# Gathering the last two chunks of four output tiles into one unit in two mixers, a gate's sigmoid from exponential and logarithm, and a bank claimed later

## The chip, the cores and the metric

The kernel runs on one core of one Trainium2 chip. The metric is the device time of one execution in microseconds; the runs of the kernel before lie at 2596.78, 2597.88 and 2606.25, with a median of 2597.88. Five engines work side by side and are tied by semaphores: TensorE (PE; its weight loads are shown as PEld), VectorE (DVE), ScalarE (ACT), GpSimd (POOL) and SyncE (SP), which issues transfers.

## The reference

Two blocks run one after the other on 512 tokens of width 1024, in float32. The first has two layers; the change touches only it.

```python
for layer in range(DEPTH):                       # DEPTH = 2
    h = modulate(rms_norm(x, mix_norm[layer]), sh1, sc1)
    y = ab_mixer(...) if layer % 2 == 0 else cd_mixer(...)
    x = x + g1 * y
    h = modulate(rms_norm(x, ffn_norm[layer]), sh2, sc2)
    x = x + g2 * swiglu(h, ffn_w1[layer], ffn_w2[layer])
# ab_mixer: four gated-linear-attention heads, four sparse attention heads
o_gla = rms_norm(o_gla, out_norm) * silu(gr)     # gr: 4 tiles of [128, 512]
return concat([o_gla, o_dsa]) @ w_out            # [512, 1024] @ [1024, 1024]
# cd_mixer: four pooled groups, four stick-breaking attention heads
return concat([o_pool, o_sb]) @ w_out            # the same shape
```

## The kernel before, in words

**Weights.** All large weights come as one stream of units. A unit is 128 x 1024 floats (512 KB); for the output product of a mixer it holds one output tile's eight chunks of 128 x 128, one per 128 channels of the input. SP loads units in order into a ring of four slots (L1254), each after the slot's last product has raised its `emptied` semaphore. POOL splits a unit into an upper half (L1828) and a lower half (L1831). TensorE then makes each chunk as three products of 128 x 512 (`products`, L384 to L386): upper by high, upper by low, lower by high. Only after the lower half may it begin the unit.

**The output product of a mixer** (`first_mix_out`, `second_mix_out`) has eight output tiles in two passes of four, one PSUM bank for each tile of a pass. In the first pass TensorE goes over the four tiles with their first chunks while the last attention heads are still being computed; these heads are the last chunks. So all four slots of the ring are held until the last chunk of the first pass, and the first unit of the second pass is loaded and split after that. In the first mixer the chunks go in the order `MIX_ORDER = (4, 5, 0, 1, 6, 2, 3, 7)`, five of them early (`MIX_EARLY`), the other three at the end. In the second, four chunks are early, then chunks 4 and 5, then 6, then 7.

**The heads.** Steps are numbered h, two to each weight tile: `late_part(h)` (first mixer) and `sb_part(h)` (second) put attention work between the halves of a tile's products. In the first mixer, step 24 to 27 lie between the early chunks of the output product. ACT takes the gate tiles `gr` from PSUM with a Copy, and after steps 20 and 24 makes Silu of two of them each; Silu needs another table than Exp and Ln, so a table load stands before and after (`gate_silu`, `tables`). `SB_AT` and `SB_OUT_AT` say at which steps the scores and outputs of the four stick-breaking heads stand.

**Behind the product.** DVE adds each output tile to the residual (L1939), ACT squares and scales it, DVE splits it again (L1900, L1901): one chain of eight tiles. TensorE needs all eight squares in `square_sum` (L414, L416), after half of the first FFN tile. The first FFN pass has four tiles; then a loop makes the rest (`ffn`). Before this loop, in layer 0, TensorE claims bank 7 for the sums of `late_sum`. DVE frees that bank with `bias_sum` of the second pair of tiles (L1973).

## Time and profile before

| | us |
|---|---|
| median of 3 runs | 2597.88 |
| profiled execution | 2600.07 |
| its span | 2598.3 |
| TensorE busy in it | 2516.0 (97%) |
| POOL busy | 1683.6 (65%) |
| DVE busy | 1066.7 (41%) |
| ACT busy | 444.2 (17%) |

The span runs from the first to the last instruction; the profiled execution has 1.8 us around it. TensorE is the engine that is nearly always busy, so its idle stretches are what to look at. Its matmuls overlap in the record: one shows 0.39 us where the next begins 0.23 us later. `PEclk` in a row of stretches is the granted clock, where 1.00 is 2.4 GHz and 0.50 is 1.2 GHz. The first mixer's output product lies at 326 to 376 us, the second's at 897 to 965 us.

### The profile page before, as it was taken

The numbers are of one execution on the slowest core, as the hardware profiler recorded it, in microseconds if no ns is written. First come the engines' busy times: TensorE is split into PE (matmuls) and PEld (weight loads), VectorE is DVE, ScalarE is ACT, GpSimd is POOL, SyncE is SP. The second block draws the span as 40 slices with busy tenths as digits, with TensorE's granted clock in tenths as the row PEclk, the third lists the DMA queues.
The fourth block names the chain that finished last, engine by engine and source line by source line (L and its number), as shares of the span: only waits on it lengthen the run. The fifth ranks groups of instructions, "written<-read, shape, count | busy, mean of one in ns | idle before, by whom it ended". The sixth has DMA issues, their size and how long they took to land.

```text
span 2598.3 us, 31481 instructions
## 1 busy us (share of the span) xinstructions
PE 2516.0 (97%) x11763; PEld 2007.8 (77%) x11763; DVE 1066.7 (41%) x1875; ACT 444.2 (17%) x867; POOL 1683.6 (65%) x784
## 2 busy tenths in 40 slices
PE   6999999999999999999999999999999999999998
PEld 2676777888887778888888678787787887888886
DVE  5798656444337444111050023204665235431322
ACT  3213430000012420000011011013444100100000
POOL 2663366777876356777887554575444777777774
PEclk9999999999999999999999999999999999999999
DMA  6423224554532112222333211221111322222222
GB/s 235 139 73 119 76 98 152 180 189 167 201 101 81 41 65 89 97 97 97 105 135 109 76 57 58 72 97 66 49 57 50 129 97 89 97 97 97 95 95 85
DMA packets 72695, 267.27 MB, mean 103 GB/s; under 512 B 8080, under 2 KB 8352, under 8 KB 72096
## 3 DMA queue, kind: packets, MB, share of 16 engines
q1 hardware_dynamic: 59616, 214.98, 24.2%
q10 hardware_dynamic: 12992, 51.06, 5.7%
q8 instruction: 63, 1.03, 0.2%
q14 instruction: 24, 0.20, 0.0%
HBM read 261.81 MB, written 4.19 MB: 102 GB/s over the span
## 4 chain that ended last, share of the span: by engine, by line
PE 85%; DVE 9%; issue 3%; ACT 2%; DMA 1%; POOL 0%; SPq 0%; DVEq 0%; POOLq 0%; ACTq 0%
PE ps L384 24%; PE ps L385 23%; PE ps L386 23%; PE ps L581 1%; PE ps L583 1%; PE ps L582 1%; DVE big L2230 1%; DVE big L2229 1%; PE ps L1065 1%; PE ps L591 1%; DVE big L2388 1%; PE ps L429 1%; PE ps L1121 1%; DMA hbuf<-in_stream 1%; PE ps L1030 1%
## 5 line engine op out<-in xcount | busy, mean ns | idle before, releaser
L1828 POOL TENSOR_TENSOR uppers<-ring,ones 128x1024 fp32r<-128x1024 f32 x390 | 742.1, 1903 | 857.3 <-DMA ring<-in_stream 856.9
L1831 POOL TENSOR_TENSOR lowers<-ring,uppers 128x1024 fp32r<-128x1024 f32 x390 | 943.6, 2419 | 30.5
L384 PE MATMUL ps<-x_hi,uppers 128*128 128x512 f32 x1128 | 455.7, 404 | 3.2 <-DVE small L1973 3.2
L385 PE MATMUL ps<-x_lo,uppers 128*128 128x512 f32 x1128 | 441.3, 391 | 0.0
L386 PE MATMUL ps<-x_hi,lowers 128*128 128x512 f32 x1128 | 441.2, 391 | 0.0
L384 PE MATMUL ps<-h_hi,uppers 128*128 128x264 f32 (+1 forms) x832 | 287.9, 346 | 2.9 <-DVE od_lo L2586 2.3
L384 PE MATMUL ps<-hid,uppers 128*128 128x512 f32 x736 | 290.1, 394 | 0.0
L386 PE MATMUL ps<-hid,lowers 128*128 128x512 f32 x736 | 286.7, 390 | 0.0
L385 PE MATMUL ps<-hid,uppers 128*128 128x512 f32 x736 | 286.4, 389 | 0.0
L385 PE MATMUL ps<-h_lo,uppers 128*128 128x264 f32 (+1 forms) x832 | 281.2, 338 | 0.0
L386 PE MATMUL ps<-h_hi,lowers 128*128 128x264 f32 (+1 forms) x832 | 280.2, 337 | 0.0
L384 PEld LDWEIGHTS ps<-x_hi,uppers 128*128 128x128 f32 x1128 | 213.2, 189 | 55.8 <-issue 12.7
L385 PEld LDWEIGHTS ps<-x_lo,uppers 128*128 128x128 f32 x1128 | 213.0, 189 | 49.7 <-issue 6.7
L386 PEld LDWEIGHTS ps<-x_hi,lowers 128*128 128x128 f32 x1128 | 213.0, 189 | 45.3
L1274 ACT ACTIVATE gate<-ps 128x512 f32<-128x512 f32 (+3 forms) x136 | 75.9, 561 | 864.8 <-PE ps L386 707.5
L384 PEld LDWEIGHTS ps<-h_hi,uppers 128*128 128x128 f32 x832 | 159.1, 191 | 30.2 <-issue 9.0
L385 PEld LDWEIGHTS ps<-h_lo,uppers 128*128 128x128 f32 x832 | 158.9, 191 | 17.8 <-issue 1.0
L386 PEld LDWEIGHTS ps<-h_hi,lowers 128*128 128x128 f32 x832 | 158.8, 191 | 16.4
L385 PEld LDWEIGHTS ps<-hid,uppers 128*128 128x128 f32 x736 | 138.3, 188 | 29.3 <-issue 1.0
L386 PEld LDWEIGHTS ps<-hid,lowers 128*128 128x128 f32 x736 | 138.1, 188 | 29.2
L384 PEld LDWEIGHTS ps<-hid,uppers 128*128 128x128 f32 x736 | 138.2, 188 | 29.0 <-issue 1.0
L2084 DVE TENSOR_TENSOR ps<-gate,ps 128x512 f32<-128x512 f32 x40 | 27.9, 696 | 289.2 <-PE ps L386 289.2
(338 smaller groups left out, 3252.9 us busy)
## 6 DMA issues: line engine op xcount, KB each, us to landing
ring<-in_stream SPq DMA_DIRECT2D x390, 512.0 KB, 3.2
sq<-in_ada_late ACTq DMA_DIRECT2D x20, 512.0 KB, 3.2
rs<-in_ada_late ACTq DMA_DIRECT2D x20, 512.0 KB, 4.9
big<-in_ada_late ACTq DMA_DIRECT2D x16, 512.0 KB, 4.2
big<-in_stream SPq DMA_DIRECT2D x12, 512.0 KB, 17.1
gate<-in_ada_rest ACTq DMA_DIRECT2D x12, 512.0 KB, 3.2
big<-in_ada_rest ACTq DMA_DIRECT2D x12, 512.0 KB, 3.9
hbuf<-in_stream SPq DMA_DIRECT2D x4, 512.0 KB, 8.5
```

Source lines behind the costliest of these rows:

```text
L384: pe.matmul(out, upper, hi, start=start, stop=False)
L385: pe.matmul(out, upper, lo, start=False, stop=False)
L386: return pe.matmul(out, lower, hi, start=False, stop=stop)
L429: pe.matmul(ps[:, bank, 2 * (n % 2):2 * (n % 2) + 2], w[:, s, k * P:(k + 1) * P], shift_halves[:, k, :], start=k == 0 and w is uppers, sto ...
L581: pe.matmul(out, hi[:, at], upper, start=k == 0, stop=False)
L582: pe.matmul(out, hi[:, at], lower, start=False, stop=False)
L583: mm = pe.matmul(out, lo[:, at], upper, start=False, stop=k == KC - 1)
L591: pe.matmul(ps[:, b, 0:n], ones[:, :], src, start=True, stop=True).then_inc(full[b], 1)
L1274: return act.activation(out, in_, func, **kw)
L1828: pool.tensor_tensor(uppers[:, s, :], w, ones[:, 0:1].broadcast_to((P, UNIT)), ALU.mult)\
L1831: pool.tensor_tensor(lowers[:, s, :], w, uppers[:, s, :].bitcast(F32), ALU.subtract)\
L2084: tt(u, g, u, ALU.mult).then_inc(sem(st + "_hidden"), 1)
```

## The change

1. **Gathered units.** For each of the two output products one unit is added to the ring, between the first pass's four and the second pass's four. It holds the last two chunks of the four tiles of the first pass: 4 tiles x 2 chunks x 128 columns. SP fills it with four transfers of 128 KB (`gather`); the fourth waits for the first three to land. The four units of the first pass are loaded whole as before, but their slots are released after the sixth chunk. Then `last_chunks` makes the last two chunks of all four tiles from the gathered unit. The first three tiles report by a semaphore of their own (`_first_y`), the fourth by the slot's.
2. **Order in the first mixer.** Five chunks of a tile as before, then the sixth of tiles 0, 1, 2 behind the third tile, and that of tile 3 behind the fourth. In the second mixer chunks 4 and 5 stand where they stood.
3. **Gates.** silu(g) becomes g * exp(min(g, 0) - ln(1 + exp(-|g|))). ACT makes Abs, Exp, Ln in the step of the old Copy (`gate_log`) and Exp in the next (`gate_sigmoid`); DVE makes one operation in each of these steps (`gate_sum`, `gate_out`), and frees the bank with the second. All stay in one table.
4. **Late bank.** The wait for bank 7 moves from before the FFN loop to the place in the loop where `late_sum` first writes it.
5. **First stick-breaking head.** Its scores and its outputs stand one step later (12 to 13, 16 to 17).

```diff
-MIX_EARLY = 5
+MIX_EARLY = 6
-SB_AT = (12, 18, 22, 26)
-SB_OUT_AT = (16, 22, 26, 30)
+SB_AT = (13, 18, 22, 26)
+SB_OUT_AT = (17, 22, 26, 30)
...
+            def out_units(st, uname, columns):
+                base = state["u"]
+                stream(uname, 0, NT)
+                gathered[base + NT] = (len_units() - NT, columns)
+                stream(uname, NT, NT)
+                state["u"] += NT + 1
...
+            def last_chunks(st, order, halves, chunk=lambda n: n):
+                s = unit()
+                for x, n in enumerate(order):
+                    pe.wait_ge(sem(st + "_split"), n + 1)
+                    for q in range(4):
+                        mm = products(ps[:, q, :], s, 2 * q + x, *halves(chunk(n)), False, n == KC - 1)
+                        if n == KC - 1:
+                            mm.then_inc(sem(st + "_first_y") if q < 3 else emptied[s], 1)
...
             def second_mix_out():
                 for n in range(2):
                     sb_part(28 + n)
                     for q in (2 * n, 2 * n + 1):
-                        chunks(0, q, range(4, 6))
+                        out_chunks("m1", q, slot_of(units_of[q]), range(4, 6), cd_halves).then_inc(emptied[units_of[q] % RING], 1)
                 sb_part(30)
-                for q in range(4):
-                    chunks(0, q, range(6, 7))
-                for q in range(4):
-                    chunks(0, q, range(7, 8)).then_inc(emptied[(loop["base"] + q) % RING], 1)
+                last_chunks("m1", range(6, 8), cd_halves)
...
             def ffn(st, layer):
                 if layer == 0:
-                    claim(7, "late", True)
+                    late_bank = nuse[7]
+                    uses["late"] = (7, late_bank)
+                    nuse[7] += 1
                 with pe.Fori(1, FF // 2) as i:
...
                     if layer == 0:
+                        pe.wait_ge(drained[7], late_bank)
                         late_sum(i - 1)
...
             def first_mix_out():
                 for q in range(4):
                     late_part(2 * len(LATE_TILES) + q)
                     take(0, q)
-                    slot(0, q)
-                    chunks(0, q, range(MIX_EARLY))
-                for q in range(4):
-                    chunks(0, q, range(MIX_EARLY, KC)).then_inc(emptied[(loop["base"] + q) % RING], 1)
+                    out_chunks("m0", q, slot_of(units_of[q]), range(MIX_EARLY - 1), mix_halves, order)
+                    for p in {2: (0, 1, 2), 3: (3,)}.get(q, ()):
+                        out_chunks("m0", p, units_of[p] % RING, (MIX_EARLY - 1,), mix_halves, order)\
+                            .then_inc(emptied[units_of[p] % RING], 1)
+                last_chunks("m0", range(MIX_EARLY, KC), mix_halves, order)
...
+            def gather(n, u):
+                s = u % RING
+                at, columns = gathered[u]
+                sp.wait_ge(emptied[s], u // RING)
+                for q in range(4):
+                    if q == 3:
+                        sp.wait_ge(sem("gathered"), 48 * (n + 1))
+                    out = ring[:, s, q * 2 * P:(q + 1) * 2 * P].rearrange("p (k c) -> p k c", c=P)
+                    of = columns(stream_dram[at + q, :, :].rearrange("p (k c) -> p k c", c=P))
+                    sp.dma_start(out, of).then_inc(filled[s] if q == 3 else sem("gathered"), 16)
...
-            def gate_silu(t):
-                was_drained(act, ("gr", t))
-                f(L0["gr"][:, t, :], L0["gr"][:, t, :], ACT.Silu).then_inc(sem("gla_gate"), 1)
+            def gate_log(t):
+                v = rs[:, 0, :]
+                b = ready(act, ("gr", t))
+                was_drained(act, ("gr", t - 1) if t else ("qk", QK_TILES[-1]))
+                link(f(v, ps[:, b, :], ACT.Abs))
+                link(f(v, v, ACT.Exp, scale=-1.0))
+                f(v, v, ACT.Ln, bias=one_col).then_inc(sem("gr_log"), 1)
+            def gate_sigmoid(t):
+                act.wait_ge(sem("gr_sum"), t + 1)
+                f(rs[:, 0, :], rs[:, 0, :], ACT.Exp).then_inc(sem("gla_gate"), 1)
...
-                if h in (20, 24):
-                    for t in range((h - 20) // 2, (h - 20) // 2 + 2):
-                        gate_silu(t)
-                    tables()
...
+            def gate_sum(t):
+                v = rs[:, 0, :]
+                dve.wait_ge(sem("gr_log"), t + 1)
+                stt(v, ps[:, uses[("gr", t)][0], :], 0.0, v, ALU.min, ALU.subtract).then_inc(sem("gr_sum"), 1)
+            def gate_out(t):
+                dve.wait_ge(sem("gla_gate"), t + 1)
+                drain_link(tt(L0["gr"][:, t, :], ps[:, uses[("gr", t)][0], :], rs[:, 0, :], ALU.mult), ("gr", t))
```

How the instructions stand, at three places. First SP's queue. Before, all ring loads of the program are these rows of one loop, a slot's wait and its load:

```order
L1254 ISA [waits emptied0]
L1254 DMA ring<-in_stream 128x1024
L1254 ISA [waits emptied1]
L1254 DMA ring<-in_stream 128x1024
L1254 ISA [waits emptied2]
L1254 DMA ring<-in_stream 128x1024
L1254 ISA [waits emptied3]
L1254 DMA ring<-in_stream 128x1024
```

Now the loop ends before the first mixer's output product, where two single loads, the four pieces of the gathered unit and one more load stand (L1289 is a whole unit, L1300 a piece) before the next loop:

```order
L1309 COMPARE_AND_BRANCH
L1289 DMA ring<-in_stream 128x1024 [waits emptied0]
L1289 DMA ring<-in_stream 128x1024 [waits emptied1]
L1300 DMA ring<-in_stream 128x2x128 [waits emptied2]
L1300 DMA ring<-in_stream 128x2x128 x2
L1300 DMA ring<-in_stream 128x2x128 [waits gathered]
L1289 DMA ring<-in_stream 128x1024 [waits emptied3]
L1309 UNCONDITIONAL_BRANCH
```

The load of the next slot, which waited for its own slot alone, now stands behind a piece that waits for the first three to land. In the second mixer the four pieces read 128x256 instead of 128x2x128.

Second TensorE at the end of the first FFN pass of layer 0 and the start of the loop, before:

```order
L385 MATMUL ps<-hid,uppers 128x512
L386 MATMUL ps<-hid,lowers 128x512
L689 UNCONDITIONAL_BRANCH [waits drained7]
L689 ISA
L605 REGISTER_ALU [waits drained0]
L384 MATMUL ps<-x_hi,uppers 128x512 [waits x_normed,lower_made2]
L385 MATMUL ps<-x_lo,uppers 128x512
```

and now:

```order
L389 MATMUL ps<-hid,uppers 128x512
L390 MATMUL ps<-hid,lowers 128x512
L730 UNCONDITIONAL_BRANCH
L730 ISA
L644 REGISTER_ALU [waits drained0]
L388 MATMUL ps<-x_hi,uppers 128x512 [waits x_normed,lower_made3]
L389 MATMUL ps<-x_lo,uppers 128x512
```

The wait for bank 7 at the branch is gone. It stands now at the end of each pass of the loop, ahead of the sums that write the bank:

```order
L390 MATMUL ps<-x_hi,lowers 128x512
L713 ISA [waits drained7]
L715 ISA [waits late_read1]
L715 MATMUL ps<-ones,consts 128x1
L715 ISA
L715 MATMUL ps<-ones,consts 128x1
```

Third ACT in steps 20 and 21 of the first mixer; `rs<-ps,small` and `rs<-rs` without `gr_sum` or `act_chain` are the root of a head's norm, 128x128 from `ps` is an output of the sparse attention that leaves its bank. Before:

```order
L1274 ACTIVATE big<-ps 128x512 [waits emptied3]
L1274 ACTIVATE big<-ps 128x384 [waits full4]
L1274 ACTIVATE big<-big 128x128 [waits dsa_max]
L1274 ACTIVATE rs<-ps,small 128x512 [waits full6,gla_normed]
L1274 ACTIVATE rs<-rs 128x512 [waits drained6]
L1274 ACT_TABLE_LOAD
L1274 ACTIVATE big<-big 128x512 [waits drained2]
L1274 ACTIVATE big<-big 128x512 [waits drained3]
L1294 ACT_TABLE_LOAD
L1274 ACTIVATE big<-ps 128x128 [waits full4]
```

and now:

```order
L1339 ACTIVATE big<-ps 128x128 [waits full4]
L1339 ACTIVATE rs<-ps 128x512 [waits drained2,emptied3]
L1339 ACTIVATE rs<-rs 128x512 [waits act_chain]
L1339 ACTIVATE rs<-rs,small 128x512 [waits act_chain]
L1339 ACTIVATE big<-ps 128x384 [waits full4]
L1339 ACTIVATE big<-big 128x128 [waits dsa_max]
L1339 ACTIVATE rs<-ps,small 128x512 [waits full6,gla_normed]
L1339 ACTIVATE rs<-rs 128x512 [waits drained6]
L1339 ACTIVATE big<-ps 128x128 [waits full4]
L1339 ACTIVATE rs<-rs 128x512 [waits gr_sum]
L1339 ACTIVATE big<-ps 128x512 [waits full4]
L1339 ACTIVATE big<-big 128x256 [waits dsa_max]
```

The two table loads and the two Silu between the root and the next output are gone; the Copy of a gate tile has become three operations in `rs`, and one Exp follows behind the output.

## Rows read from the trace of the kernel before

**Rows 1.** The page's busy time, share of the span and instructions, of TensorE

```profile
PE 2516.0 (97%) x11763; PEld 2007.8 (77%) x11763; DVE 1066.7 (41%) x1875; ACT 444.2 (17%) x867; POOL 1683.6 (65%) x784
```

**Rows 2.** TensorE's waits, whole span: us in total, times, longest us

```profile
PE ps L384 <- POOL lowers L1831: 7.6, 2, 5.8
...
PE ps L933 <- ACT big L1274: 4.5, 2, 2.7
...
PE ps L384 <- DVE small L1973: 3.2, 1, 3.2
...
PE ps L497 <- DVE big L2413: 2.2, 1, 2.2
```

**Rows 3.** TensorE in time: start, us, operation, idle before; first mixer, first FFN

```profile
307.01 0.66 PE L933 MATMUL ps<-consts,big 128*128 128x128 f32 x4 [2.75 <-ACT big L1274]
...
332.68 0.66 PE L933 MATMUL ps<-consts,big 128*128 128x128 f32 x4 [1.78 <-ACT big L1274]
...
337.43 0.48 PE L384 MATMUL ps<-mix_half,uppers 128*128 128x512 f32 x1
...
354.46 0.47 PE L384 MATMUL ps<-mix_half,uppers 128*128 128x512 f32 x1 [1.82 <-POOL lowers L1831]
...
376.33 0.17 PE L429 MATMUL ps<-shift_halves,uppers 128*128 128x2 f32 x1
...
410.65 0.53 PE L384 MATMUL ps<-x_hi,uppers 128*128 128x512 f32 x1 [3.25 <-DVE small L1973]
```

**Rows 4.** ACT in time, step 20 of the first mixer

```profile
302.93 1.28 ACT L1274 ACT_TABLE_LOAD   x1
...
305.39 1.28 ACT L1294 ACT_TABLE_LOAD   x1
```

**Rows 5.** Stretches: length, busy us of each engine, granted clock, DMA share, GB/s

```profile
304.00:312.00 8.00, 5.25 (x23) 4.21 (x22) 4.08 (x8) 4.17 (x9) 1.09 (x1) 0.79 0.01 2
352.00:355.00 3.00, 1.18 (x5) 0.67 (x4) 2.42 (x4) 0.51 (x1) 3.00 (x2) 1.00 0.78 255
407.00:415.00 8.00, 4.75 (x14) 3.48 (x13) 7.40 (x13) 0.72 (x1) 4.98 (x3) 0.79 0.60 197
840.00:848.00 8.00, 5.61 (x20) 4.00 (x19) 7.42 (x19) 1.22 (x4) 3.49 (x2) 0.79 0.20 66
934.00:947.00 13.00, 7.24 (x20) 5.40 (x18) 8.19 (x13) 4.49 (x8) 10.62 (x6) 0.74 0.44 159
```

**Rows 6.** POOL in time: the split of the second pass's first unit, first mixer

```profile
349.98 1.90 POOL L1828 TENSOR_TENSOR uppers<-ring,ones 128x1024 fp32r<-128x1024 f32 x1 [16.11 <-DMA ring<-in_stream]
351.96 2.36 POOL L1831 TENSOR_TENSOR lowers<-ring,uppers 128x1024 fp32r<-128x1024 f32 x1
```

**Rows 7.** DMA issues: times, KB of one, median us to landing

```profile
ring<-in_stream SPq DMA_DIRECT2D x390, 512.0 KB, 3.2
...
out<-hbuf SPq DMA_DIRECT2D x8, 256.0 KB, 2.1
```

**Rows 8.** SP in time: four issues in a row

```profile
0.75 1.94 SPq L1248 DMA_DIRECT2D hbuf<-in_stream  x4
```

**Rows 9.** DVE in time: the first two residual additions, first mixer

```profile
346.57 0.75 DVE L1939 SCALAR_TENSOR_TENSOR xres<-ps,mod,xres 128x512 f32<-128x512 f32 x1 [6.68 <-PE ps L386]
...
350.52 0.74 DVE L1939 SCALAR_TENSOR_TENSOR xres<-ps,mod,xres 128x512 f32<-128x512 f32 x1
```

**Rows 10.** TensorE in time: second mixer

```profile
843.21 0.89 PE L497 MATMUL ps<-big,consts 128*128 128x128 f32 x4 [2.25 <-DVE big L2413]
...
919.32 0.48 PE L384 MATMUL ps<-cd_half,uppers 128*128 128x512 f32 x1
...
929.14 0.48 PE L384 MATMUL ps<-cd_half,uppers 128*128 128x512 f32 x1
...
940.61 0.76 PE L384 MATMUL ps<-cd_half,uppers 128*128 128x512 f32 x1 [5.76 <-POOL lowers L1831]
...
965.40 0.17 PE L429 MATMUL ps<-shift_halves,uppers 128*128 128x2 f32 x1
```

More of the change, by code:

```diff
@@ L532, in second_mix_out @@
             def second_mix_out():
-                stream("cd_out", 0, KC)
-                slot = ring_loop(2, 4)
-                take = bank_loop(2, range(4), [("m1", "y", q) for q in range(4)])
-                def chunks(i, q, order):
-                    for k in order:
-                        if i == 0:
-                            pe.wait_ge(sem("m1_split"), k + 1)
-                        mm = products(ps[:, q, :], (loop["base"] + q) % RING, k, *cd_halves(k), k == 0, k == KC - 1)
-                    return mm
+                units_of, take = out_units("m1", "cd_out", lambda unit: unit[:, 6:8, :])
                 for n, q in enumerate((1, 2, 0, 3)):
@@ L558, in second_mix_out, with slot_of, take @@
                 for q in range(4):
                     take(1, q)
-                    s = slot(1, q)
-                    chunks(1, q, range(KC)).then_inc(emptied[s], 1)
+                    out_chunks("m1", q, unit(), range(KC), cd_halves).then_inc(emptied[(state["u"] - 1) % RING], 1)
+            def slot_of(u):
+                pe.wait_ge(lower_made[u % RING], u // RING + 1)
+                return u % RING
+            def out_units(st, uname, columns):
[4 more added lines that the diff above has]
+                state["u"] += NT + 1
+                first = {}
+                for q in range(4):
+                    name = (st, "y", q)
+                    uses[name] = (q, nuse[q])
+                    u = base + NT + 1 + q
+                    g = base + NT
+                    by_pass[name] = [(sem(st + "_first_y"), q + 1) if q < 3 else (emptied[g % RING], g // RING + 1),
+                                     (emptied[u % RING], u // RING + 1)]
+                    first[q] = nuse[q]
+                    nuse[q] += 2
+                def take(i, q):
+                    pe.wait_ge(drained[q], first[q] + i)
+                state["u"] = base + NT
+                return [base + q for q in range(NT)], take
@@ L563, in tm_group, with len_units @@
+            def len_units():
+                return sum(count for _, _, count in units)
             def tm_group(name, off, meta=None, first=4, between=None):
@@ L739, in first_mix_out @@
             def first_mix_out():
-                stream("ab_out", 0, KC)
-                slot = ring_loop(2, 4)
-                take = bank_loop(2, range(4), [("m0", "y", q) for q in range(4)])
-                def chunks(i, q, order):
-                    for n in order:
-                        if i == 0:
-                            pe.wait_ge(sem("m0_split"), n + 1)
-                        k = MIX_ORDER[n]
-                        mm = products(ps[:, q, :], (loop["base"] + q) % RING, k, *mix_halves(k), n == 0, n == KC - 1)
-                    return mm
+                units_of, take = out_units("m0", "ab_out", lambda unit: unit[:, 3::4, :])
+                order = lambda n: MIX_ORDER[n]
                 for q in range(4):
@@ L1238, in build @@
         n_first = ADA_FIRST * ADA_UNITS
-        n_ring = n_units - n_first
-        assert n_units == N_UNITS and n_ring == state["u"], (n_units, state["u"])
+        ring_at_unit = n_first
+        n_ring = n_units - ring_at_unit + len(gathered)
+        assert n_units == N_UNITS and n_ring == state["u"], (n_units, n_ring, state["u"])
         stream_dram = A["stream"]
@@ new lines, in fill_all @@
+            def fill_all(u, end, at):
+                while u < end and (u < RING or u % RING):
+                    fill(u, at)
+                    u, at = u + 1, at + 1
+                rounds = (end - u) // RING
+                if rounds:
+                    with sp.Fori(u // RING, u // RING + rounds) as i:
+                        for s in range(RING):
+                            sp.wait_ge(emptied[s], i)
+                            sp.dma_start(ring[:, s, :], stream_dram[i * RING + (at - u + s), :, :]).then_inc(filled[s], 16)
+                    u, at = u + rounds * RING, at + rounds * RING
+                while u < end:
+                    fill(u, at)
+                    u, at = u + 1, at + 1
@@ L1258, in _ @@
+            u = 0
+            for n, g in enumerate(sorted(gathered)):
+                fill_all(u, g, ring_at_unit + u - n)
+                gather(n, g)
+                u = g + 1
+            fill_all(u, n_ring, ring_at_unit + u - len(gathered))
             for k in range(KC):
@@ L1522, in _ @@
                     else:
-                        b = ready(act, (name, t))
-                        drain(f(L0["gr"][:, t, :], ps[:, b, :], ACT.Copy), b)
+                        gate_log(t)
+                elif h % 2 and 0 <= h // 2 - 1 - len(QK_TILES) < 4:
+                    gate_sigmoid(h // 2 - 1 - len(QK_TILES))
                 if h in GO_AT:
```

38 lines of the change are left out of this document (23 added, 15 removed).

## The prediction, made before the changed kernel ran

> **What bounds the kernel now.** I read the page's busy times first: TensorE is busy 2516 of 2598 us [rows 1], so only time in which it stands still, or runs at half its clock, can be won. Then I read its list of waits [rows 2]. It says how much it stood still for whom; the places are in its timeline [rows 3, 10]. Five of them lie where the change works: 2.75 and 1.78 us for ACT in the first mixer; 1.82 us there and 5.76 us in the second mixer for POOL's lower half; 3.25 us for DVE's bias sum before the FFN loop; 2.25 us for DVE in the first stick-breaking head. These are 17.6 us. The third view is the clock by stretches. A mean clock c over L us costs (1 - c) x L. Around the waits of 2.75, 3.25 and 2.25 us the stretches of 8 us have 0.79, so 1.68 us each; around the wait of 5.76 us the 13 us have 0.74, so 3.4 us, of which some 0.3 fall into the wait itself and 3.0 are lost; around the 1.82 us there is nothing, 1.00 [rows 5]. So a wait of 2.25 us or more costs 1.7 to 3.0 us beyond its own length.
>
> The unit of work below is the product of 128 x 512: 96 of them run from 354.46 to 376.33 us [rows 3], 0.228 us each.
>
> **Gates: -5.6 us.** The 2.75 us end when ACT drains an output of the sparse attention, and this drain stands behind a table load, two Silu and another load [rows 3, 4]: the loads alone are 2 x 1.28 us. The same again four steps later, 1.78 us. Now nothing stands between the root and the drain. What is added: in each of four steps two more ACT operations, one more Exp in the next step, and two operations on DVE, 0.6 to 0.75 us each at the rate of their kind (DVE's 128 x 512 addition takes 0.75 [rows 9]). ACT's longer part, some 1.3 us more, comes before it waits for TensorE's transposes of the same step, and a step's products alone last 12 x 0.228 = 2.7 us; DVE waits for scores in each of these steps. I cost them at nothing but 0.6 us (an estimate, 0.3 at each place) for the drain itself, which is what TensorE waits for now: -2.75 - 1.68 - 1.78 + 0.6 = -5.6. Bounds: -6.2 when even the drain is hidden, 0 when ACT's longer chain makes TensorE wait as long at the same places.
>
> **First mixer's output product: +4.3 us.** Here the change takes a wait of 1.82 us away and puts a new one in. Before: the first product of the third tile is at 337.43, and 66 products later, at 352.5, the first pass is over; the second pass starts at 354.46 [rows 3]. Now slot 0 comes free after 15 products of the third tile and 3 of the first: 337.43 + 18 x 0.228 + 0.15 = 341.7 (0.15 for the semaphore, and 0.1 at the hops below, are estimates). SP issues three pieces, 1.94 / 4 = 0.49 us each [rows 8], so the third goes out 1.0 us later. No row shows a transfer of 128 KB in pieces of 512 B. The nearest are 2.1 us for 256 KB, 3.2 for 512 KB [rows 7]. I take 2.1, the nearer size, with 3.2 as the upper end. The fourth piece waits for the first three: 1.0 + 2.1 + 0.1 + 2.1 = 5.3 us. POOL's split takes 1.90 + 2.36 and 0.1 between [rows 6]: 4.4. The gathered unit is ready at 341.7 + 9.6 = 351.3. TensorE gets there after 15 + 9 + 18 = 42 products, at 347.0, and waits 4.3 us. Between the stretches that rows 5 show, 1.7 and 3.0 us, I take 2.0 for the clock behind it. Then 24 products (5.5) and the second pass (21.9) end at 351.3 + 2.0 + 27.4 = 380.7, against 376.33. The second pass's own first unit is late no more: its load goes out right behind the fourth piece and lands during the split, so POOL has it ready at about 355.7, before 358.8. Bounds: +2.3 without the loss of clock; with 3.2 us for either landing 2.2 us more, and 3.0 for the clock, +7.5.
>
> By the Trainium skill, "DMA: Bandwidth & Descriptors", section "Anatomy of one DMA", a transfer costs a fixed 2.0 us plus its bytes at 436 GB/s, a fit for another issuing path. For 512 KB this gives 3.2, which is what the row has; for 128 KB it gives 2.3. The rule speaks against four pieces with a wait between them, since the fixed part is paid twice in a row; by it each mixer would come out 0.4 us later than in my sum.
>
> Who is late next: DVE's chain of residuals. The first tile is now complete at 356.9 (15 products into the gathered unit), the chain begins 10.3 us later than before [rows 9], and one link takes 350.52 - 346.57 = 3.95 us. The eighth starts at 356.9 + 7 x 3.95 = 384.6, its square is there at about 386.0. TensorE wants it at 380.7 + 1.7 + 2.7 + 0.9 = 386.0, in the second half of the square sum. So nothing is added, but the slack is used up.
>
> **Late bank: -4.9 us.** TensorE stands 3.25 us before the loop and then runs at half clock for a while, 1.68 us [rows 3, 5]. The first tile of the loop needs a bank and inputs that were ready; the third needs what DVE frees with the pair whose bias sum was waited for, and it comes 48 products, 10.9 us, after the loop's start. The new wait in the loop is met long before; it is paid only as an instruction. Bounds: -4.9 to 0, if another wait for DVE takes the place.
>
> **First stick-breaking head: -3.6 us.** At 843.21 TensorE had waited 2.25 us for DVE's first parts [rows 10], with half clock behind it, 1.68 us. One step later stand 12 products, 2.7 us, before the same operations, so DVE is ready; I leave 0.3 for its third part. The scores now come right before a pool map that waits for DVE, which is a wait in place of one of 0.78 us before them: nothing. Bounds: -3.9 to 0.
>
> **Second mixer's output product: -7.1 us.** Slot 0 is free 6 products after 919.32 [rows 10], at 920.8; with the same 9.6 us the gathered unit is ready at 930.5. TensorE has the outputs of the last head behind it at 929.3 (the next product stands at 929.14 already, the ends are modelled) and waits 1.2 us, too short for the clock by rows 5. 24 products and 96 more end at 957.9; the residual chain adds about 0.4. Before, 965.40. So the 5.76 us, and the 3.0 of clock, turn into 1.2 and 0.4. Bounds: -8.3 with no wait, -3.3 with 3.4 us of waiting and 1.7 of clock.
>
> **Sum:** -5.6 + 4.3 - 4.9 - 3.6 - 7.1 = -16.9 us. POOL's two further splits and SP's eight further issues add nothing, as TensorE's other waits for POOL are none [rows 2]. The profiled execution took 2600.07, which gives 2583; it lies 2.2 above the median of the runs, so on the median it is 2597.88 - 16.9 = 2581.
>
> By the Trainium skill, "TensorE: Matmul & The Clock Gate", section "Part 1: The HAM clock gate", the throttled clock is the default, and activity releases it. The four stretches in rows 5 agree for waits of 2.25 us and more, the one at 1.82 us shows that a short wait is free. By that rule the new wait of 4.3 us cannot be free of it; without it the sum would be -18.9.
>
> **Rivals.**
> *The gather is slow* (chance 0.20). The two landings take 3.2 us each because the pieces are many short runs. Then the first mixer pays +7.5, the second gains 3.3 and the sum is -5.6 + 7.5 - 4.9 - 3.6 - 3.3 = -9.9: 2588. For it: no row shows such a piece. Against it: half the size of the 2.1 us row.
> *The removed waits come back on DVE and ACT* (0.16). Four gates bring ACT some 1.9 us in a row and DVE 1.4 us each, and the FFN loop may wait for the pair after all. If the gates give 1.5, the late bank 3.2 (its wait, not its clock), and the first head nothing, the sum is -1.5 + 4.3 - 3.2 - 7.1 = -7.5: 2590. Against it: DVE is busy 41% [rows 1].
> *The new waits are cheap* (0.10). No loss of clock in the first mixer and no wait in the second: -16.9 - 2.0 - 1.2 = -20: 2578.
> *Slower than before* (0.05). The mechanism is the gather alone: every microsecond of a landing beyond 2.1 is paid four times, twice in each mixer, and with the clock (3.4 us more in all) the gain of 16.9 is used up from a landing of 2.1 + 13.5 / 4 = 5.5 us on. At 9 us each the time would be about 2612. The rows' 3.2 us for four times the bytes speak against it.
> *The change doesn't do what it says* (0.04): the slots are released early, but the loads of the second pass stand behind the fourth piece on SP and the ring has nothing for TensorE anyway. Then the first mixer loses as in the slow gather and the second stays as it is: -5.6 + 7.5 - 4.9 - 3.6 = -6.6: 2591.
>
> **How the numbers follow.** The forecast has 0.45. Its own range is 2577 to 2586. A measurement of this kernel tells about 0.5%, 13 us, from no change, which puts the limit at 2584.9. The forecast falls below it 9 times in 10, the cheap rival always, the slow gather 3 in 20, the DVE rival hardly: 0.41 + 0.10 + 0.03 + 0.02 = 0.56, and I say 0.57. Slower by as much has 0.04, within it 0.39. The range for 8 in 10 reaches from the cheap rival to the DVE rival: 2575 to 2591.
>
> **What would show it.** TensorE's waits for ACT at the transposes (2.75, 1.78) gone, and the granted clock at 1.00 through the steps behind them. A new wait for POOL of 3 to 6.5 us before the first gathered unit, with half clock behind it, and one of 0 to 3.4 us in the second mixer; SP's three issues, then a gap of 2 us, then one. No wait before the FFN loop and none of DVE's at its third and fourth tile. It would be wrong if a landing of a piece is well off 2.1 us, if the wait for the gathered unit in the second mixer is over 2 us, or if DVE is waited for in steps 20 to 25.

## The result, and the profile of the changed kernel

| | before | changed |
|---|---|---|
| median, us | 2597.72 | 2605.64 |
| runs | 20 | 20 |
| ratio, 95% interval | | 1.003 (1.0022 to 1.0038) |
| profiled execution, us | 2600.07 | 2609.14 |
| its span, us | 2598.3 | 2607.3 |

The changed kernel is 8 us slower; 17 us faster was forecast, and the time lies above the range of 2575 to 2591. One execution of all, the profiled one of the first head alone, ran at a clock of 0.555 throughout (4218.56 us), and it is in no ratio below. TensorE's busy time has gone up by 5.9 us against [rows 1], and since it executes the same number of instructions, that is time at half clock:

```profile
PE 2521.9 (97%) x11763; PEld 2011.7 (77%) x11763; DVE 1087.7 (42%) x1883; ACT 443.1 (17%) x871; POOL 1692.2 (65%) x788
```

Its list of waits (us in total, times, longest) answers to [rows 2]. The wait for the DVE bias sum (3.2) is gone and the transposes wait 0.4 for ACT where they waited 4.5. In their place stands one that the prediction doesn't have: L433, the bias sums of the first FFN tile (L429 before), for a DVE sum of squares (L1983), once in each mixer. POOL is waited for nearly as long as before.

```profile
PE ps L433 <- DVE big L1983: 7.7, 2, 4.2
PE ps L388 <- POOL lowers L1901: 7.2, 2, 5.5
...
PE ps L388 <- DVE xres L2009: 1.8, 1, 1.8
PE ps L515 <- DVE big L2508: 1.8, 1, 1.8
...
PE ps L967 <- ACT big L1339: 0.4, 1, 0.4
```

**A ledger of offsets.** Both kernels give TensorE the same 11763 matmuls (86 of them, at the first stick-breaking head, in another order), so I laid the two traces side by side by instruction and took the difference of the start times, changed minus before. Where it jumps, an engine waited or was spared a wait; where it ramps, one of the two ran at half clock.

| stretch | offset from, to (us) | measured | prediction's term |
|---|---|---|---|
| steps before the gates | 0, +1.3 | +1.3 | 0 |
| gates | +1.3, -2.9 | -4.2 | -5.6 |
| first mixer's output product | -2.9, +3.5 | +6.4 | +4.3 |
| between it and the square sum | +3.5, +11.95 | +8.4 | 0 |
| FFN loop entered (late bank) | +11.95, +6.85 | -5.1 | -4.9 |
| first stick-breaking head | +6.85, +6.2 | -0.7 | -3.6 |
| second mixer's output product, to its second pass | +6.2, +3.0 | -3.1 | -7.1 (with the next) |
| between it and the square sum | +3.0, +9.8 | +6.8 | in the -7.1 |
| rest of the program | +9.8, +9.0 | -0.8 | 0 |

Two stretches of 15.2 us, for which I had 0.4, are the largest part of the error: 14.8 of the 25.9 us between -16.9 and +9.0. The first 1.3 us are of no part of the change: the stretch of 8 us from 238 ran at 0.79 in this execution and at 1.00 in the one before.

The first of the two stretches in TensorE's timeline (start, us, operation, idle before) answers to the 354.46 and 376.33 of [rows 3]:

```profile
349.80 0.80 PE L388 MATMUL ps<-mix_half,uppers 128*128 128x512 f32 x1 [5.48 <-POOL lowers L1901]
...
357.99 0.39 PE L388 MATMUL ps<-mix_half,uppers 128*128 128x512 f32 x1
...
384.12 0.34 PE L433 MATMUL ps<-shift_halves,uppers 128*128 128x2 f32 x1 [4.21 <-DVE big L1983]
...
392.79 1.09 PE L418 MATMUL ps<-big,ones 128*128 128x512 f32 x2
```

TensorE waits 5.48 us for the gathered unit and starts the second pass 3.5 us later than before. It ends it at 379.9, and then stands until 384.12. The clock by stretches (length, PE busy, granted clock, DMA share, GB/s) has the price of both waits: full clock through the pass, 0.55 behind each wait.

```profile
349.80:356.00 6.20, 6.20 (x16) 0.55 0.00 0
357.99:380.00 22.01, 21.92 (x97) 1.00 0.29 96
380.00:384.00 4.00, 0.00 (x0) 0.83 0.41 131
384.00:394.00 10.00, 9.88 (x31) 0.55 0.00 0
```

What DVE did meanwhile, its timeline shows, against [rows 9]:

```profile
356.12 0.75 DVE L2009 SCALAR_TENSOR_TENSOR xres<-ps,mod,xres 128x512 f32<-128x512 f32 x1 [19.08 <-PE ps L390]
358.15 0.69 DVE L1970 CAST hid<-ps 128x512 fp32r<-128x512 f32 x1 [1.28 <-ACT ps L1339]
...
360.08 0.74 DVE L2009 SCALAR_TENSOR_TENSOR xres<-ps,mod,xres 128x512 f32<-128x512 f32 x1
...
383.18 0.68 DVE L1983 TENSOR_TENSOR big<-ps,sq 128x512 f32<-128x512 f32 x1
383.78 0.74 DVE L2009 SCALAR_TENSOR_TENSOR xres<-ps,mod,xres 128x512 f32<-128x512 f32 x1
```

The chain starts at 356.12 (346.57 before), every link takes the 3.95 us that it took, and the eighth residual starts at 383.78. The prediction had 356.9, 3.95 and 384.6. The chain's arithmetic was right to 0.8 us; what TensorE wants of it, and when, was not. The first FFN tile begins with bias sums that go to bank 4, and bank 4 holds DVE's running sum of squares until the seventh (383.18, 0.68 long). TensorE follows 0.3 us behind its end.

In the second mixer the same, with a bank in addition: the second pass cannot start before the first residual has drained its bank.

```profile
937.24 0.50 PE L388 MATMUL ps<-cd_half,uppers 128*128 128x512 f32 x1 [1.68 <-POOL lowers L1901]
...
944.83 0.50 PE L388 MATMUL ps<-cd_half,uppers 128*128 128x512 f32 x1 [1.82 <-DVE xres L2009]
...
972.02 0.24 PE L433 MATMUL ps<-shift_halves,uppers 128*128 128x2 f32 x1 [3.52 <-DVE big L1983]
```

There the chain starts late by itself. The first tile's last product ends at about 941.0, but the first residual starts at 944.03, since DVE still has four operations before it:

```profile
936.23 1.24 DVE L2480 CAST cd_half<-big 128x512 fp32r<-128x512 f32 x1 [3.85 <-ACT big L1339]
937.50 2.26 DVE L2481 TENSOR_TENSOR cd_half<-big,cd_half 128x512 fp32r<-128x512 f32 x1
939.69 2.36 DVE L1957 SCALAR_TENSOR_TENSOR coef<-mod,vecs 128x8 f32<-128x8 f32 x1
942.08 1.82 DVE L1962 CAST shift_halves<-mod 128x8 fp32r<-128x8 f32 x1
```

They take 7.7 us. In the kernel before the same four took 0.43, 0.69, 0.16 and 0.17, while POOL stood idle; here POOL splits without a pause from 937.22 on. What this collision is, the runs with POOL held show below. In the first mixer the chain has no such delay: the residual at 356.12 follows the tile's last product at once.

The gather itself, on SP and POOL (first mixer):

```profile
338.92 4.53 SPq L1300 DMA_DIRECT2D ring<-in_stream  x4
343.49 0.60 SPq L1289 DMA_DIRECT2D ring<-in_stream  x1
```

```profile
345.44 1.89 POOL L1898 TENSOR_TENSOR uppers<-ring,ones 128x1024 fp32r<-128x1024 f32 x1 [13.69 <-DMA ring<-in_stream]
347.41 2.34 POOL L1901 TENSOR_TENSOR lowers<-ring,uppers 128x1024 fp32r<-128x1024 f32 x1
```

```profile
ring<-in_stream SPq DMA_DIRECT2D x8, 128.0 KB, 2.4
```

From the first issue to the split 6.5 us, where the prediction had 5.3; a piece lands in 2.4 us in the median of the eight, 2.6 in this stretch (taken: 2.1).

### The profile page after: what moved, and what is told of

The parts are those of the page before. It is cut to its first block, busy times and chain, and to the rows that moved or that the text cites. A ratio compares the mean times of both kernels' runs of the same rounds, so it can differ in the third digit from the quotient of the medians.

```text
span 2607.3 us, 31487 instructions
## 1 busy us (share of the span) xinstructions
PE 2521.9 (97%) x11763; PEld 2011.7 (77%) x11763; DVE 1087.7 (42%) x1883; ACT 443.1 (17%) x871; POOL 1692.2 (65%) x788
## 4 chain that ended last, share of the span: by engine, by line
PE 86%; DVE 9%; ACT 2%; issue 1%; DMA 1%; POOL 0%; SPq 0%; DVEq 0%; ACTq 0%
PE ps L388 24%; PE ps L389 23%; PE ps L390 23%; PE ps L620 2%; PE ps L622 2%; PE ps L621 2%; DVE big L2300 1%; DVE big L2299 1%; PE ps L1099 1%; PE ps L433 1%; PE ps L630 1%; ACT big L1339 1%; DMA hbuf<-in_stream 1%; PE ps L1155 1%; PE ps L1064 1%
## 5 line engine op out<-in xcount | busy, mean ns | idle before, releaser
L389 PEld LDWEIGHTS ps<-h_lo,uppers 128*128 128x128 f32 x832 | 158.4, 190 | 17.8 <-issue 1.0
```

The lines of the kernel that those rows point to most:

```text
L389: pe.matmul(out, upper, lo, start=False, stop=False)
```

## The experiments

Ratios are to the kernel before on the same chip, with 95% intervals; a difference in us beside a ratio is worked out from the ratio, not from the medians. Theory A is that the gather costs through DVE's chain of residuals.

### One part of the change at a time

Four kernels, each the kernel before with one part of the diff shown above.

*The gathered units alone* (parts 1 and 2):

> Kernel before plus part 1 and 2 alone (gathered units in both mixers), nothing else changed. Theory A (the residual chain): in the changed kernel no tile of the first pass is complete until the gathered unit's last chunk, so DVE's chain of eight residuals starts some 9.5 us later in the first mixer, and TensorE, which needs seven of its squares already before the bias sums of the first FFN tile, waits 4.2 us there and loses 4.2 us of clock; in the second mixer 3.6 and 3.2. By the offsets between the two traces the gather costs 14.8 us in the first mixer and 3.7 in the second: +18.5 us, 2616. Theory B (the gather itself is what costs, the rest of the 8 us being parts 3 to 5 that do not pay): +6.3 in the first mixer, -7 in the second, about 2597, with the loss to be found in the other kernels of this job. Theory C (my prediction): -2.8, 2595.

Measured: 1.0071 (1.0053 to 1.0089), +18.4 us. By offsets to before the trace has +17.8 behind the second mixer, of which 1.0 arose before the first edited place; over the whole span it is +15.0. The waits are those of the changed kernel: 5.5 and 2.2 us for POOL, 4.2 and 3.5 at the bias sums. The loss is all in the gather; theories B and C are out.

*The gates alone* (part 3):

> Kernel before plus part 3 alone (sigmoid from exponential and logarithm). Theory A: the two waits of 2.75 and 1.78 us for ACT before the sparse attention's transposes go, 2.9 us net at the first (with its clock 4.3) and 1.3 net at the second, where the changed kernel lost 1.3 us to half clock in between: -4.2 us, 2593.5. Theory B (the loss is in the parts other than the gather): 0 to +3 us. Prediction's term: -5.6, 2592.

Measured: 0.9976 (0.9966 to 0.9987), -6.2 us; -5.5 by the trace's offsets. The prediction's -5.6 was right; the changed kernel's -4.2 has 1.3 us of half clock at 318 to 326 in it, which this trace has not.

*The late bank alone* (part 4):

> Kernel before plus part 4 alone (the late sums' bank waited for inside the FFN loop). Theory A: the 3.25 us before the loop and the clock behind it go and nothing comes in their place, as the traces of the changed kernel show: -5.1 us, 2592.6. Theory B (wait comes back at the third tile of the loop): -1 to 0.

Measured: 0.9992 (0.9979 to 1.0005), -2.1 us. The interval reaches from -5.5 to +1.3, so this run alone decides nothing. In its trace the wait before the loop is gone and none has come in its place.

*The first head alone* (part 5):

> Kernel before plus part 5 alone (scores and outputs of the first stick-breaking head one step later). By the traces the waits of 2.25 and 0.78 us are replaced by four of 0.95, 0.61, 0.66 and 1.80 us: -0.7 us, 2597. Prediction's term: -3.6, 2594. A rival: the wait of 1.80 us for DVE before the outputs belongs to this part alone, so that the part costs a little, +0.5.

Measured: 1.0003 (0.9991 to 1.0014), +0.8 us: no gain, as in the changed kernel. It has no trace that can be laid beside the others.

The four add up to +10.9 us, against +7.9 measured for the whole, a difference that their intervals allow.

### The chain

*Bias sums behind the first tile's products*, with the gathered units alone:

```diff
-                    for k in range(KC):
-                        for w in (uppers, lowers):
-                            pe.matmul(ps[:, bank, ...], ..., shift_halves[:, k, :], ...)
+                    if n: shift_sums()
...
+                if shifted and n == 0:
+                    pe.wait_ge(sem("shift_split"), shift_uses[st])
+                    mm = shift_sums()
```

> The kernel with the gathered units alone, and the bias sums of the first FFN tile moved from before its products to behind them. Then TensorE needs the seventh sum of squares only after 12 products (2.7 us later), and works on the inputs that are there. Theory A (TensorE waits for DVE's chain, and the place of that wait is the first thing of the FFN tile): the wait of 4.2 us becomes 1.3 for the seventh and 1.1 for the eighth square, with less half clock behind it; in both mixers together -4 to -8 us against gather only: ratio to before 1.004 to 1.0055. Theory B (the cost sits in the gather's landing and split): unchanged, 1.007.

Measured: 1.0048 (1.0031 to 1.0064), 6.0 us less than the gather alone, though the two intervals overlap. The wait left there is that of the square sum:

```profile
PE ps L418 <- DVE big L1979: 2.1, 2, 1.4
```

7.7 us have become 2.1, by giving TensorE 12 products to do before it asks; this the trace shows more sharply than the time. So the place where it asks was the error, and it is the seventh sum of squares that it lacks, no data of the tile.

*A shorter chain*, with the gathered units alone. The split and the sum of squares of tile k move behind the residual of tile k + 1:

```diff
-                    if raw is not None and (held is None or k == KC - 1):
-                        raw_split(st, k, *raw(k))
-                    if k < KC - 1:
-                        sum_square(st, k)
+                    late = 5 if layer is not None and raw is not None and held is None else 0
+                    for j in (...):   # k < 5: k - 1;  k == 5: k - 1, k;  then k
+                        raw_split(st, j, *raw(j)) ... sum_square(st, j)
```

> The kernel with the gathered units alone, and DVE's chain of residuals in another order for its first five links: the residual of tile k + 1 comes before the split and the sum of squares of tile k, so that DVE no longer stands 1.28 us for ACT in a link, and a link takes 2.7 to 2.8 us in place of 3.95. The gather and its landing are untouched. Theory A: the chain has caught up with the tiles by the sixth, the wait before the first FFN tile and the half clock behind it go in both mixers, 8.4 + 6.8 = 15 us: ratio 1.0013, about +3 us against before. Theory B (the wait for DVE is only a symptom and the time comes back elsewhere): 1.005 or more.

Measured: 1.0006 (0.9995 to 1.0016). DVE's timeline, links two and three:

```profile
365.29 0.74 DVE L2001 SCALAR_TENSOR_TENSOR xres<-ps,mod,xres 128x512 f32<-128x512 f32 x1
365.95 0.68 DVE L1962 CAST hid<-ps 128x512 fp32r<-128x512 f32 x1
366.66 0.69 DVE L1963 TENSOR_TENSOR hid<-ps,hid 128x512 fp32r<-128x512 f32 x1
367.27 0.69 DVE L1975 TENSOR_TENSOR ps<-ps,sq 128x512 f32<-128x512 f32 x1
367.87 0.74 DVE L2001 SCALAR_TENSOR_TENSOR xres<-ps,mod,xres 128x512 f32<-128x512 f32 x1
...
383.06 0.68 DVE L1975 TENSOR_TENSOR big<-ps,sq 128x512 f32<-128x512 f32 x1
385.13 0.75 DVE L2001 SCALAR_TENSOR_TENSOR xres<-ps,mod,xres 128x512 f32<-128x512 f32 x1 [1.40 <-PE ps L390]
```

A link takes 2.58 us and has no wait for ACT in it, up to the fifth; by the eighth tile DVE waits for TensorE, as in the kernel before. The wait at L433 is not in the list, and the gather has come down from +18.4 to +1.6 us, with its transfers untouched. That shows the chain as the cause: 16.8 us by the ratios, give or take 5. The traces say it more exactly. The two stretches behind the passes are +8.2 and +5.3 us in the gather alone, and -0.1 and 0.0 here. The wait of 1.8 us for the second mixer's bank has stayed.

*The last chunks tile by tile*, with the gathered units alone:

```diff
-                for x, n in enumerate(order):
-                    pe.wait_ge(sem(st + "_split"), n + 1)
-                    for q in range(4):
+                for q in range(4):
+                    for x, n in enumerate(order):
+                        pe.wait_ge(sem(st + "_split"), n + 1)
```

> The kernel with the gathered units alone, with both last chunks of a tile made one behind the other, tile by tile, in place of chunk by chunk over four tiles. The first tile is complete after 6 products and not 15, so the chain starts 2.1 us earlier at full clock and up to 3.8 at half clock. Theory A: in the first mixer the wait of 4.2 us shrinks to under 1 and its clock loss goes, in the second the wait of 3.6 shrinks to 1.5 and the wait of 1.8 for the first bank shrinks too: -9 to -12 us against gather only, ratio 1.003. Theory B: 1.007.

Measured: 1.0059 (1.0043 to 1.0075), only 3 us less than the gather alone, less than the intervals can tell apart: a miss in size. In the traces the first mixer gains 4.3 us and the second loses 1.7. The L433 waits went from 7.7 to 4.9 us, but in the second mixer the eighth chunk, the last head, is now asked for three products into the unit instead of twelve:

```profile
939.80 0.50 PE L388 MATMUL ps<-cd_half,uppers 128*128 128x512 f32 x1 [2.33 <-POOL lowers L1893]
942.38 0.79 PE L388 MATMUL ps<-cd_half,uppers 128*128 128x512 f32 x1 [1.62 <-DVE cd_half L2462]
```

*The whole change with the shorter chain:*

> The whole change, and DVE's chain of residuals in the shorter order of the run before (residual of tile k + 1 ahead of the split of tile k, for the first five). Theory A: the 8.4 and 6.8 us behind the two passes go, so 1.003 becomes 0.9970 to 0.9975, about 2591. Theory B: over 1.000.

Measured: 0.9981 (0.9969 to 0.9992). 12.7 us come back; the change is then faster than before. The expected 0.9970 to 0.9975 are at the interval's lower edge.

### The combination, and a second cause

*Gates, late bank, short chain, and a gathered unit in the second mixer alone, filled by one transfer:*

```diff
-                for q in range(4):
-                    ... sp.dma_start(out, of).then_inc(filled[s] if q == 3 else sem("gathered"), 16)
+                out = ring[:, s, :].rearrange("p (q c) -> p q c", q=4)
+                of = stream_dram[at:at + 4, :, 6 * P:8 * P].rearrange("q p c -> p q c")
+                sp.dma_start(out, of).then_inc(filled[s], 16)
```

> Gates and late bank as in the change, first stick-breaking head as before, the gathered unit in the second mixer only and filled by one transfer of 512 KB in place of four pieces, and the short chain of the run before. Theory A: gates -6.2, late bank -2 to -5, second mixer -3.1 without the chain's 6.8, and with one landing in place of two in a row the wait of 1.7 us for POOL goes too: -13 to -16 us, ratio 0.994 to 0.995. Theory B (chain not the cause): the second mixer gains nothing, ratio 0.9965.

Measured: 0.9966 (0.9952 to 0.998), theory B's number. But the wait at the bias sums is gone, so what was lost here was not lost to the chain. The offsets are -8.9 until the last head's outputs and then lose 8.3 us within 10. There TensorE waits for DVE, and DVE, whose timeline is next, takes 5.93 us for four multiplications by the mask:

```profile
915.56 0.69 DVE L2508 TENSOR_TENSOR big<-big,ps 128x512 f32<-128x512 f32 x1 [4.35 <-PE ps L504]
916.16 5.93 DVE L2515 TENSOR_TENSOR big<-big,consts 128x128 f32<-128x128 f32 x4
```

In the kernel before the same four take 1.08 us. What is new beside them is POOL's split of the gathered unit:

```profile
915.60 1.90 POOL L1903 TENSOR_TENSOR uppers<-ring,ones 128x1024 fp32r<-128x1024 f32 x1 [22.03 <-DMA ring<-in_stream]
917.57 2.48 POOL L1906 TENSOR_TENSOR lowers<-ring,uppers 128x1024 fp32r<-128x1024 f32 x1
```

*The same with POOL held* until DVE has multiplied:

```diff
+                hold[base + NT] = (sem("sb_w"), 16)      # the gathered unit
...
+                    if rest + n + RING * it == u:
+                        pool.wait_ge(*hold[u])
                     split_unit(...)
```

> The best combination so far, with POOL held before it splits the gathered unit until DVE has multiplied the last head's four weight tiles by the mask. In the run before, POOL's split began 0.6 us ahead of them, and the four multiplications, 1.08 us in the kernel before, took 5.93; TensorE waited 4.0 us for them and ran at half clock behind. Theory P (POOL's split and a DVE operation with two SBUF inputs block each other): the four take 1.1 us again, the gathered unit is ready 1.6 us later and costs a wait of 1.3 or so; 6 us are won against the run before, ratio 0.994 to 0.9945. Theory Q (the four were slow for another cause, such as the transfers that landed at the same time): they stay near 6 us, and the ratio is 0.9965 or above.

Measured: 0.995 (0.9936 to 0.9963), 2585.04 us.

```profile
913.30 1.08 DVE L2529 TENSOR_TENSOR big<-big,consts 128x128 f32<-128x128 f32 x4
```

```profile
914.46 1.89 POOL L1905 TENSOR_TENSOR uppers<-ring,ones 128x1024 fp32r<-128x1024 f32 x1 [23.67 <-DVE big L2529]
```

Theory P holds: with the transfer as it was and only the split moved, the four take 1.08 us. TensorE's wait of 4.0 us is gone; one of 1.3 for the unit has come. The gain over the run before is 4 us by the ratios and 5.8 by the medians, where I had expected 6; the intervals overlap, and over the second mixer the two traces differ by 5.3. What the hold doesn't reach stays: the four operations before the first residual still take 7.3 us beside the splits that follow, and TensorE waits 1.85 us for that residual's bank. No run holds POOL there. By the Trainium skill, "SBUF — State Buffer", section "Who interferes with whom", a VectorE instruction with two SBUF inputs contends with a GpSimd instruction that reads SBUF, and the later one blocks. The trace agrees: one multiplication takes 0.28 us alone and up to 2.43 beside a split, and the first of the four, begun at 916.16, ends at 917.64, right behind POOL's first half (917.50).

*The first head alone, POOL held* before the unit that meets its multiplications. In the changed kernel these stood beside a split too, and the head's outputs waited 1.80 us:

```profile
860.52 4.21 DVE L2508 TENSOR_TENSOR big<-big,consts 128x128 f32<-128x128 f32 x4
```

```profile
859.92 1.89 POOL L1898 TENSOR_TENSOR uppers<-ring,ones 128x1024 fp32r<-128x1024 f32 x1 [4.07 <-DMA ring<-in_stream]
```

The edit is the hold above, with `sem("sb_w"), 4` for that unit.

> Kernel before plus part 5 alone (first stick-breaking head one step later), with POOL held before the one unit whose split falls on DVE's mask multiplications of that head. In the changed kernel these four took 4.21 us against 1.07 before, and TensorE waited 1.80 us before the head's outputs. Theory P: they take 1.1 us, that wait is gone, and the part gives -1.5 to -3 us, near the prediction's term. Theory Q: 4 us again.

Measured: 0.9996 (0.9986 to 1.0006). The time can't tell it from nothing or from the run without the hold. The trace can: the four are short, the 1.80 us are gone, and the offset to before goes from -1.35 to -4.0 over the head, -2.65 where the changed kernel had -0.7.

```profile
852.40 1.07 DVE L2442 TENSOR_TENSOR big<-big,consts 128x128 f32<-128x128 f32 x4
```

*Gates and late bank alone:*

> Kernel before plus gates and late bank, with neither gather nor the first head's shift. By the two single runs -6.2 and -2.1 (by the traces -5.8 and -5.1): ratio 0.9957 to 0.997.

Measured: 0.9955 (0.9942 to 0.9969), 2587.96 us. Two small edits give all but 0.0005 of the best combination, and in time the two can't be told apart (2587.96 and 2585.04 us, five runs each).

*The best combination with the first head* (its shift and its hold):

> e11 and in addition the first stick-breaking head one step later with POOL held before the unit that collides with its mask multiplications. By the trace of e12 (offset to before -1.35 us ahead of the head, -4.0 behind it) this gives -2.7 us against e11: ratio 0.9940. If the part is worth nothing, 0.995 as e11.

Measured: 0.9957 (0.9941 to 0.9974), no better than without. Its trace has the shortest span of all (2576.8 us), and -2.6 us over the head, but one execution doesn't outweigh the five runs.

*The pieces at once*, with the gathered units alone and the short chain. The fourth piece no longer waits on SP; POOL waits for all four:

```diff
-                    if q == 3:
-                        sp.wait_ge(sem("gathered"), 48 * (n + 1))
...
+                hold[base + NT] = (sem("gathered"), 48 * (len(gathered) + 1))
```

> The gathered units alone with the short chain (as e6), but the fourth piece is issued right behind the third, and POOL waits for all four. In the changed kernel POOL had the unit 6.5 us after the first issue: three issues, a landing of 2.6, then the fourth's landing. If the two landings in a row are what the first mixer pays for, POOL begins 4.0 to 4.6 us after the first issue, TensorE's wait of 5.5 us falls to about 3.5, that of 1.7 in the second mixer goes: -3 to -4 us against e6, ratio 0.9990 to 0.9995. If the landing is bound by the bytes or by other transfers, nothing: 1.0006.

Measured: 1.0019 (1.0007 to 1.0032), not below the 1.0006 of the run it is compared with. POOL does begin 4.8 us after the first issue (345.11) in place of 6.7, and TensorE waits 3.7 us in place of 5.6:

```profile
349.89 1.89 POOL L1890 TENSOR_TENSOR uppers<-ring,ones 128x1024 fp32r<-128x1024 f32 x1 [13.49 <-DMA ring<-in_stream]
```

But up to the first mixer's second pass this trace loses 4.9 us and the other 5.5: the clock gives 3.0 us away behind the shorter wait and 1.7 behind the longer. In the second mixer the earlier split falls on the mask multiplications (2.58 us for four), and this trace gains 3.7 us where the other gains 3.0. So the earlier landing was worth 0.6 and 0.7 us in the traces, where 3 to 4 were expected. Why the clock took more is open, and so is whether the 3 us by which this kernel is slower than the other are real: the intervals overlap, and in its one trace 2.5 us arise at 84 us, in work that the edit doesn't touch.

## Why the prediction was wrong

**The step that failed** is "Who is late next". It says that TensorE wants the eighth square "at 380.7 + 1.7 + 2.7 + 0.9 = 386.0, in the second half of the square sum. So nothing is added". The 1.7 are the bias sums, and I let them run first. In the code they wait for the seventh sum of squares, because DVE's partial sum lies in the bank that they write (`raw_tile`, the wait on `x_summed` ahead of the shift matmuls). So TensorE wants the chain at 379.9, not 386.0, and gets it at 384.1. The description of the kernel before has the same error: it names the square sum as the first place that needs the chain. The same line in the second mixer, "the residual chain adds about 0.4", stood on the same error. Together they measured 15.2 us by the ledger, and 16.8 by the ratios when the chain was shortened; without them the change runs at 0.9981.

**Gates, -5.6:** right. Alone -6.2 in time and -5.5 in the trace.

**First mixer's output product, +4.3:** right in its mechanism, 2.1 too small: 5.48 us of waiting where I had 4.3 (pieces of 2.4 to 2.6 us instead of 2.1, which was the row of a store, `out<-hbuf`, and not of a load), 2.7 of clock where I had 2.0. That is inside its bounds. By the Trainium skill, "DMA: Bandwidth & Descriptors", section "Anatomy of one DMA", the fit for another issuing path makes an estimate of 2.3 us for such a piece; the 2.4 measured are nearer to that than to the row that I took.

**Late bank, -4.9:** right by the traces (-5.1), with nothing in its place. In time it hardly shows: 0.9992 alone, whose interval includes no change at all, and 0.9955 together with the gates against 0.9976 for the gates alone, whose intervals touch. Its clock part isn't safe either: with the gathered units and the short chain, without this edit, the same wait of 3.27 us stood at 419.28, and the 8 us around it had 1.00 where [rows 5] have 0.79.

**First head, -3.6:** mis-sized, -0.7. I priced the operations at their durations elsewhere. One step later they meet a split of POOL's, and four multiplications take 4.21 us instead of 1.07. With the split out of their way the trace gives -2.65, and the time still can't tell it from nothing.

**Second mixer, -7.1:** its first half was right in kind. The wait of 5.76 us became one of 1.68, as predicted (1.2). I left out the bank of the second pass's first tile (1.82 us), which the first residual frees, and the clock behind it. That residual is 3 us later than its tile, because the new unit's split and the next fall on the four operations of DVE ahead of it (7.7 us instead of 1.5); so some 3 us of the chain's lateness in this mixer are of that kind too. This is an estimate from the durations in the two traces. -3.1 instead of -7.5 up to the second pass, and then the chain.

**Its sums.** 5.3 and 4.4 us give 9.7, not 9.6. The range was said to reach from the cheap rival to the DVE rival, which are at 2578 and 2590, and was written as 2575 to 2591. Neither matters here. The row from which short waits were read as free ends 0.5 us behind the wait; [rows 3] bear the reading out for that place, with 0.228 us for each of the 96 products behind it, but it was one place.

**The rivals.** None of them was it. The slower rival named the gather and a landing of 5.5 us or more; the gather it was, but with landings of 2.4 us. The chain had been worked out to the microsecond and set aside with "the slack is used up". A slack that is used up to zero on a path whose place is only assumed should have been a rival with a price.

## What to carry to other kernels

Where a change delays the first result of a serial chain on a helper engine, find the first wait of the main engine on that chain in the code, not the place where its data is needed: a shared buffer can make an unrelated first instruction wait. When a chain has become late, look for a wait for a third engine inside its links; doing the next link's first operation there took this one from 3.95 to 2.58 us. Work moved in time should be laid beside what the other engines do there, since a duration taken from a quiet stretch didn't hold beside POOL's splits: 7.7 us for four operations that had taken 1.5.

## What the hardware showed that I had not expected

- DVE's multiplication of 128x128 with both inputs in SBUF takes 0.28 us, and up to 2.45 beside POOL's split; with POOL held back it takes 0.28 again. An operation of 128x8 (`coef<-mod,vecs`) with both inputs in SBUF went from 0.16 to 2.36 us in the same way.
- A wait's price in clock doesn't go by its length. The wait of 1.82 us at 944.83 is followed by 8 us at 0.79, that of the same length in [rows 5] by 1.00. The first had another wait, of 1.68 us, 5.8 us ahead of it; whether that is the reason no run tests. A wait of 3.7 us was followed by 3.0 us of lost clock, one of 5.6 by 1.7, and one of 3.25 before the FFN loop by 1.7 in the kernel before and by none in the short chain's run. The rule that I read from [rows 5], that short waits are free, doesn't hold.
- Half clock also comes without any long wait, in one execution and not in the next: 238 to 246 us ran at 0.79 in the changed kernel and at 1.00 before, with the same instructions.
